# Four ring tiles in place of eight, and a selection step moved behind the last product row

## The chip, the cores and the metric

The kernel runs on one core of a Trainium2 chip. The metric is the device time of one execution in microseconds (us), the median of several runs. The core has five engines, each with its own instruction stream: TensorE (PE, its weight loads shown as PEld), VectorE (DVE), ScalarE (ACT), GpSimd (POOL) and SyncE (SP). They meet only at semaphores. Data come from HBM by DMA; here POOL issues the gathers and SP the weight loads, and the 16 DMA engines of the core carry both.

## The reference

One inference step of a two-layer decoder, for 256 prompt tokens and 32 sample tokens (288 in all, width 1024). Layer 0 mixes tokens by a short gated convolution, layer 1 by an RWKV-7 recurrence. Behind each mixer stands the same expert step, and the change lies in it alone:

```python
q = (hc @ wq).reshape(-1, 8, 256)                 # 8 heads
s1, s2 = q[..., :128] . k1,  q[..., 128:] . k2    # 128 keys each
v1, i1 = top_k(s1, 16);  v2, i2 = top_k(s2, 16)
sc, ci = top_k(v1[:, None] + v2[None, :], 16)     # 16 of 256 pairs
eidx = e1 * 128 + e2                              # one of 16384 experts
gate = softmax(sc)
z = gelu(einsum('cd,chkd->chk', hc, u_tab[eidx]))
return einsum('chk,chkd->cd', gate * z, v_tab[eidx])
```

For every token, head and choice one row of 1024 numbers is fetched from the table U and one from the table V (4 KB each). That is 288 x 8 x 16 x 2 rows in each layer.

## The kernel before

**Units.** A unit is 128 pairs of a token and a head, one per partition. Each layer has 18 units: 8 for each of two tiles of 128 prompt tokens, and 2 for the sample tokens. For a unit, choice k (0 to 15) is one gather of 128 rows of U and one of 128 rows of V, half a megabyte each. So a layer has 288 U gathers and 288 V gathers.

**Rings.** U tiles land in the ring RU, V tiles in RVV. Each holds RING = 8 tiles; choice k goes to slot k % RING. Every slot has a semaphore that says it has landed (u_land, v_land).

**The five streams of the expert step.** Unit u is the one whose V rows are in work; its U rows were handled one unit earlier, so the loops work on V of unit u beside U of unit u+1.

- POOL (L1872, get_u and get_v) issues the gathers in one fixed order: V(u,0), U(u+1,0), V(u,1), U(u+1,1), and so on. Before V(u,k) it waits until the product that used the slot last is done (v_free), before V(u,0) also for the unit's V indices (s_vidx); before U(u+1,k) it waits until the row product that used the slot last is done (s_z), before U(u+1,0) for that unit's selection (s_sel). At a layer's start it fetches the 16 U tiles of the first unit and the first RING of the second one, and then it alternates.
- DVE (unit, L1479 and on) does the row product z_of (L1449): 1024 products and their sum for each partition, of the U row and the token's h. Between the z of unit u+1 it runs the selection of unit u+2, the generator choose: 13 pieces of two instructions (maxima, indices, the grid of 256 sums), and a 14th that normalizes the gates: it waits for ACT's exponential (s_gexp), sums 16 numbers (L1429), takes the reciprocal (L1430) and scales (L1431). Two pieces stand behind each z with k = 1 to 7, so the 14th stands behind z 7. Before z 8 DVE writes the V indices of unit u+1 (v_indices, L1444). coef (L1505) multiplies gate and gelu, for 8 choices at a time.
- ACT (unit, L1098 and on) scales the V rows by their coefficients (L1114), one instruction of 128 x 1024 for each tile, in the order of k. At a unit's start it copies the scores of unit u+2 (L1104) and takes the gelu of the second eight z of unit u (L1095), before k = 10 the gelu of the first eight z of unit u+1, and before k = 13 the exponential for the gates of unit u+2 (gate_exp, L1064).
- PE (unit, L642 and on) turns each scaled V tile and adds it up in PSUM: 8 transposing products of 128 x 128 per tile (L646), and counts v_free up.
- After units 7, 15 and 17 of a layer DVE empties the PSUM sums (tile_out, L1519 and L1523).

**Around it.** SP loads weights into a ring W of its own. In layer 0 the loads for the next mixer (in_rwkv_wr) wait for the end of the last selection and so run beside the last units. The last unit has V rows alone.

Of the kernel before, what the change touches and what calls it, by code (L numbers as in the profile page):

```python
# [12 lines left out]
P = 128  # L13
D = 1024
# [4 lines left out]
TOK = NP_TOK + NS_TOK  # L19
# [3 lines left out]
HEADS = 8  # L23
NKEYS = 128
NEXP = NKEYS * NKEYS
TOPK = 16
UNITS = 18
RING = 8
WRING = 4
BANKS = 4  # L30
NEG = -3.0e38
# [88 lines left out]
def build(nc, a, out):  # L120
    with ExitStack() as ctx:
        def sb(name, shape, dt=F32):
            return ctx.enter_context(nc.sbuf_tensor(name, [P] + list(shape), dt))
# [20 lines left out]
        W = sb("W", [WRING, DC, 512])  # L144


        N_RV, N_ROWS, N_SEL = 2 * RING * D, 3 * D, 2880
        ARENA = sb("ARENA", [N_RV + 2 * N_ROWS + N_SEL])
        RV = ARENA[:, 0:N_RV]
        HTOK = ARENA[:, N_RV:N_RV + N_ROWS].rearrange("p (a d) -> p a d", a=3)  # L150
# [8 lines left out]
        gsm = sb("gsm", [2, 2])  # L159
        COUT = sb("COUT", [DC, 18])  # L160

        rings = RV.rearrange("p (r s d) -> p r s d", r=2, s=RING)
        RU, RVV = rings[:, 0], rings[:, 1]

        def carve(off, shape, dt=F32):
            n = int(np.prod(shape))
            v = ARENA[:, off:off + n]
            if dt is not F32:
                v = v.bitcast(dt)
            names = " ".join("abcd"[:len(shape)])  # L170
            return v.rearrange(f"p ({names}) -> p {names}", **{"abcd"[i]: s for i, s in enumerate(shape)})
# [12 lines left out]
        CS = carve(2 * DC * TOK + DC * UHW + DC * TOK, [DC * NS_TOK])  # L184
        CROW = carve(N_RV + N_ROWS, [D])

        KR = [carve(off, [2, HEADS, P]) for off in (RING * D + 2560, RING * D + 512)]

        Q = carve(RING * D, [16, TOK])
        KT = carve(RING * D + 16 * TOK, [2, HEADS, NKEYS])  # L190

        QP = carve(N_RV + N_ROWS, [16, P])
        HS4 = carve(N_RV + N_ROWS + 16 * P, [DC, P])
# [101 lines left out]
        s_vidx = sem("v_indices_ready")  # L295
        u_land = [sem(f"u_landed{i}") for i in range(RING)]
        v_land = [sem(f"v_landed{i}") for i in range(RING)]
# [166 lines left out]
        def _(pe):  # L464
# [72 lines left out]
            def turn_keys(layer):  # L537
                pe.wait_ge(s_keys, 16 * 2 * (layer + 1))
                for i in range(4):
                    o = group(f"kt{layer}", i)  # L540
                    for j in range(4):
                        m = pe.transpose(o[:, j * P:(j + 1) * P], KR[layer][:, i // 2, 4 * (i % 2) + j, :], ident[:])
                    done(m)
# [37 lines left out]
            def experts(layer):  # L581
# [21 lines left out]
                for h in range(2):  # L603
                    for half in range(2):
                        m = pe.matmul(o[:, (2 * h + half) * P:(2 * h + half + 1) * P], Q[:, 2 * h + half, 0:P], KT[:, half, h, :],
                                      start=True, stop=True)
# [5 lines left out]
                for tile in range(2):  # L612
                    for half in range(2):
                        for h4 in range(2):
                            o = group(f"sc{layer}", n)
                            n += 1
                            for j in range(4):
                                h = 4 * h4 + j
                                m = pe.matmul(o[:, j * P:(j + 1) * P], Q[:, 2 * h + half, tile * P:(tile + 1) * P],  # L619
                                              KT[:, half, h, :], start=True, stop=True)  # L620
                            done(m)
# [312 lines left out]
        def _(act):  # L934
# [9 lines left out]
            def load_keys(layer):  # L944
                for half, k in enumerate(("peer_k1", "peer_k2")):
                    act.dma_start(KR[layer][:, half, :, :], a[k][layer].rearrange("h k d -> k h d")).then_inc(s_keys, 16)

# [97 lines left out]
            def experts(layer):  # L1045
                squares(2 * layer + 1)
                root_and_h(2 * layer + 1)
                if layer == 0:
                    ada("ad3")
                for i in range(2):  # L1050
                    copy(f"hf{layer}", i, HTOK[:, 0, i * 512:(i + 1) * 512])

                def query(m):
                    o, free = take(f"qa{layer}", m) if m < 4 else take(f"qb{layer}", m - 4)
                    act.activation(Q[:, m, :], o[:, 0:TOK], ACT.Copy).then_inc(s_q, 1)  # L1055
                    act.wait_ge(s_q, 16 * layer + m + 1)
                    act.sem_inc(free, 1)

                u0 = layer * UNITS

                def gate_exp(u, e):

                    act.wait_ge(s_sel, u * NSEL + SEL_IDX)
                    act.activation(GATE[:, e, :], GATE[:, e, :], ACT.Exp).then_inc(s_gexp, 1)  # L1064

                for m in range(4):
                    query(m)
                o, free = take(f"se{layer}", 0)
                for e in range(2):
                    act.activation(SCUR[:, e].rearrange("p a k -> p (a k)"), o[:, 2 * e * P:2 * (e + 1) * P], ACT.Copy).then_inc(s_scur, 1)  # L1070
                act.wait_ge(s_scur, u0 + 2)
                act.sem_inc(free, 1)
                for m in range(4, 16):
                    query(m)
                    if m == GEXP_AT[0]:
                        gate_exp(u0, 0)
                    if m == GEXP_AT[1]:
                        gate_exp(u0 + 1, 1)

                for n in range(8):  # L1080
                    tile, half, h4 = n // 4, (n // 2) % 2, n % 2
                    copy(f"sc{layer}", n, SCALL[:, 8 * tile + 4 * h4:8 * tile + 4 * h4 + 4, half * NKEYS:(half + 1) * NKEYS],
                         lambda o: o.rearrange("p (h k) -> p h k", h=4))
                copy(f"sc{layer}", 8, SCALL[:, 16:18, :].rearrange("p e (a k) -> p a e k", a=2),
                     lambda o: o.rearrange("p (a e k) -> p a e k", a=2, e=2))
                for tile in range(1, 3):
                    for i in range(2):
                        copy(f"ht{layer}", 2 * tile - 2 + i, HTOK[:, tile, i * 512:(i + 1) * 512])
                for j in range(9):
                    taken(f"sc{layer}", j)  # L1090

                def gelu(u, e, half):
                    h = slice(8 * half, 8 * half + 8)
                    act.wait_ge(s_z, u * 16 + (8 * half + 8))
                    act.activation(GL[:, e, h], ZB[:, e, h], ACT.Gelu).then_inc(s_gelu, 1)  # L1095

                gelu(u0, 0, 0)

                def unit(u, lu, e, last):
                    if last == 0:  # L1100

                        act.wait_ge(s_sel, u * NSEL + NSEL)
                        act.sem_inc(s_actgo, 1)
                        act.activation(SCUR[:, e].rearrange("p a k -> p (a k)"), at(SCALL, lu + 2), ACT.Copy).then_inc(s_scur, 1)  # L1104
                    gelu(u, e, 1)
                    for k in range(TOPK):
                        if k == 10 and last < 2:
                            gelu(u + 1, 1 - e, 0)
                        if k == 13 and last == 0:
                            gate_exp(u + 2, e)  # L1110
                        if k % 8 == 0:
                            act.wait_ge(s_coef, u * 2 + (k // 8 + 1))
                        act.wait_ge(v_land[k % RING], u * 32 + 16 * (k // RING + 1))
                        act.activation(RVV[:, k % RING, :], RVV[:, k % RING, :], ACT.Copy, scale=CF[:, e, k:k + 1]).then_inc(s_scaled, 1)  # L1114

                with act.Fori(0, UNITS // 2 - 1) as i:
                    for e in range(2):
                        unit(i * 2 + (u0 + e), i * 2 + e, e, 0)
                for e in range(2):
                    unit(u0 + UNITS - 2 + e, UNITS - 2 + e, e, 1 + e)  # L1120
# [132 lines left out]
        def _(v):  # L1253
# [84 lines left out]
            for c in range(DC):  # L1338
# [5 lines left out]
                for j in range(3):  # L1344
                    k = col("conv_k", 8 * j + c)
# [88 lines left out]
            def experts(layer):  # L1434
# [10 lines left out]

                def z_of(u, k, e, h):

                    v.wait_ge(u_land[k % RING], u * 32 + 16 * (k // RING + 1))
                    v.scalar_tensor_tensor(RU[:, k % RING, :], RU[:, k % RING, :], 1.0, h, ALU.mult, ALU.mult,  # L1449
                                           accum_out=ZB[:, e, k:k + 1]).then_inc(s_z, 1)  # L1450

# [26 lines left out]
                def unit(u, lu, e, last):  # L1478

                    chosen = choose(u + 2, e, layer) if last == 0 else iter(())  # L1480
                    if last < 2:
                        for k in range(TOPK):
                            if k == 3:
                                coef(u, e, 1)
                            if k == 8:

                                v.wait_ge(s_sel, u * NSEL + 2 * NSEL)
                                v.wait_ge(v_free, u * 16 + RING)
                                v_indices(1 - e)
                            z_of(u + 1, k, 1 - e, at(HTOK, (lu + 1) // 8))  # L1490
                            if k == 14:
                                coef(u + 1, 1 - e, 0)
                            if 1 <= k < 8 or k == 15:
                                next(chosen, None)
                                next(chosen, None)
                    else:
                        coef(u, e, 1)
                    for _ in chosen:
                        pass
# [448 lines left out]
```

## Time and profile before

| | us |
|---|---|
| median of 3 runs | 2758.37 (2747.98 to 2760.15) |
| the profiled execution, its own time | 2752.55 |
| its span | 2750.8 |
| PE, DVE, POOL, ACT busy | 1985.1, 1364.6, 1311.3, 1031.9 |
| gathers, POOL's queue | 165888 packets, 604.05 MB |

Busy shares over the whole span mix stages. The two expert steps take about 840 us each (the first V gather of layer 0 starts at 326.3 us and the last at 1138.6, in layer 1 at 1909.1 and 2719.7); in them POOL and the DMA engines are busy nearly all the time, DVE and PE a good half. A row of the timeline gives start, duration, engine, line, operation and, in brackets, the idle time before it and what ended it; "issue" there is a gap in which the engine waited for nothing that the profile shows.

### The profile page before, as it was taken

What the parts mean: (1) busy time and instruction counts of PE and PEld (TensorE: products, weight loads), DVE (VectorE), ACT (ScalarE), POOL (GpSimd) and SP (SyncE); (2) the same over time, 40 slices, a digit from 0 to 9 for tenths busy, and PEclk for the clock granted to TensorE, in tenths of its full rate; (3) what the DMA queues carried; (4) which work ended last, traced back from release to release, by engine and by line L of the source; (5) the groups of instructions that cost most, each with busy time, mean ns of one, the idle gap of its engine ahead of it and who ended that gap; (6) DMA issues with size and microseconds to landing.
All of it is one profiled execution on the core that took longest, in us unless ns stands there. A gap on an engine that the chain in (4) does not pass through costs nothing.

```text
span 2750.8 us, 32207 instructions
## 1 busy us (share of the span) xinstructions
PE 1985.1 (72%) x10179; PEld 1594.1 (58%) x10179; DVE 1364.6 (50%) x3386; ACT 1031.9 (38%) x1308; POOL 1311.3 (48%) x1216
## 2 busy tenths in 40 slices
PE   6998865666666665698589897898656666666666
PEld 3676754544545544576389896567444555455455
DVE  1032655465655655323752624726465656556552
ACT  2202344444444444513211111223444444454545
POOL 2000677777777777300000000006777777777774
PEclk8899965565555555799689897899656555555556
DMA  9743899999999999724100002427999999999996
GB/s 359 289 153 124 287 363 329 361 365 367 337 360 351 367 360 392 293 95 168 38 1 1 1 1 76 115 67 249 350 347 361 351 372 347 360 362 364 356 351 243
DMA packets 242654, 717.42 MB, mean 261 GB/s; under 512 B 39672, under 2 KB 45056, under 8 KB 242556
## 3 DMA queue, kind: packets, MB, share of 16 engines
q0 software_dynamic: 165888, 604.05, 59.4%
q1 hardware_dynamic: 62212, 105.00, 10.9%
q10 hardware_dynamic: 14456, 7.06, 1.0%
q8 instruction: 61, 1.00, 0.1%
q14 instruction: 37, 0.30, 0.0%
HBM read 712.38 MB, written 3.65 MB: 260 GB/s over the span
## 4 chain that ended last, share of the span: by engine, by line
PE 35%; DMA 18%; issue 17%; DVE 13%; POOL 10%; ACT 6%; POOLq 0%; DVEq 0%; ACTq 0%; SPq 0%
PE ps L557 14%; DMA ARENA<-in_peer_v,CURV 13%; POOL ARENA L1872 10%; DVE ARENA L1449 7%; PE ps L646 5%; PE ps L774 5%; DMA ARENA<-in_peer_u,CURU 3%; ACT ARENA L1114 2%; ACT L1064 1%; PE ps L534 1%; PE ps L756 1%; PE ps L520 1%; DMA W<-in_w_ada 1%; PE ps L510 1%; PE ps L619 1%
## 5 line engine op out<-in xcount | busy, mean ns | idle before, releaser
L646 PE MATMUL ps<-ident,ARENA 128*128 128x128 f32 x4608 | 1023.3, 398 | 617.5 <-ACT ARENA L1114 616.6
L646 PEld LDWEIGHTS ps<-ident,ARENA 128*128 128x128 f32 x4608 | 833.4, 209 | 807.5 <-ACT ARENA L1114 788.3
L1872 POOL DMA_INDIRECT ARENA<-in_peer_u,CURU x576 | 642.2, 1115 | 1174.2 <-DVE ARENA L1424 978.2
L1114 ACT ACTIVATE ARENA<-ARENA,CF 128x1024 f32<-128x1024 f32 x576 | 658.1, 1147 | 769.8 <-DMA ARENA<-in_peer_v,CURV 766.6
L1449 DVE SCALAR_TENSOR_TENSOR ARENA<-ARENA 128x1024 f32<-128x1024 f32 x576 | 686.6, 1223 | 185.1 <-DMA ARENA<-in_peer_u,CURU 183.5
L1872 POOL DMA_INDIRECT ARENA<-in_peer_v,CURV x576 | 653.1, 1134 | 230.6 <-issue 152.3
L557 PE MATMUL ps<-H,W 128*128 128x288 f32 x1024 | 255.0, 412 | 3.5 <-DVEq L1801 2.8
L1429 DVE TENSOR_REDUCE gsm<-ARENA 128x1 f32<-128x16 f32 x36 | 6.1, 170 | 472.5 <-ACT ARENA L1064 472.5
L557 PEld LDWEIGHTS ps<-H,W 128*128 128x128 f32 x1024 | 197.7, 194 | 58.8 <-DVEq L1801 3.0
L967 ACT ACTIVATE W<-ps 128x512 f32<-128x512 f32 (+2 forms) x97 | 55.8, 577 | 231.4 <-PE ps L774 171.4
L967 ACT ACTIVATE ARENA<-ps 128x512 f32<-128x512 f32 (+4 forms) x106 | 55.0, 541 | 201.7 <-PE ps L557 85.2
L774 PE MATMUL ps<-W 128*128 128x128 f32 (+1 forms) x1088 | 127.6, 282 | 0.1
L557 PE MATMUL ps<-ARENA,W 128*128 128x288 f32 x512 | 127.4, 412 | 0.0
L774 PEld LDWEIGHTS ps<-W 128*128 128x128 f32 (+1 forms) x1088 | 125.5, 196 | 2.3 <-issue 0.9
L557 PEld LDWEIGHTS ps<-ARENA,W 128*128 128x128 f32 x512 | 98.7, 193 | 27.5
L1730 DVE TENSOR_TENSOR W<-W,ps 128x512 f32<-128x512 f32 (+1 forms) x76 | 50.6, 666 | 72.1 <-PE ps L774 71.3
L756 PE MATMUL ps<-ARENA 64*128 64x128 f32 (+1 forms) x480 | 59.6, 312 | 23.7 <-DVEq L1263 22.0
L756 PEld LDWEIGHTS ps<-ARENA 64*128 64x128 f32 (+1 forms) x480 | 52.5, 212 | 30.7 <-DVEq L1263 27.1
L520 PE MATMUL ps<-W,CTZ 128*32 128x512 f32 x384 | 59.4, 756 | 7.1 <-DMA W<-in_w_ada 7.1
L1552 DVE SCALAR_TENSOR_TENSOR ARENA<-ARENA,PAR,H 128x288 f32<-128x288 f32 x48 | 21.8, 514 | 82.1 <-PE ps L557 81.1
L1055 ACT ACTIVATE ARENA<-ps 128x288 f32<-128x288 f32 x32 | 13.1, 409 | 93.5 <-PE ps L557 93.3
L1449 DVE DVE_READ_ACCUMULATOR ARENA<-ARENA 128x1 f32 x576 | 46.8, 81 | 0.0
(282 smaller groups left out, 1657.6 us busy)
## 6 DMA issues: line engine op xcount, KB each, us to landing
W<-in_w_ada SPq DMA_DIRECT2D x24, 2048.0 KB, 12.6
W<-in_peer_wq SPq DMA_DIRECT2D x8, 2048.0 KB, 8.2
W<-in_conv_w_in SPq DMA_DIRECT2D x6, 2048.0 KB, 12.3
ARENA<-in_peer_u,CURU POOLq DMA_INDIRECT x576, 6.3
ARENA<-in_peer_v,CURV POOLq DMA_INDIRECT x576, 6.2
W<-in_conv_w_out SPq DMA_DIRECT2D x2, 2048.0 KB, 7.9
W<-in_rwkv_wr SPq DMA_DIRECT2D x2, 2048.0 KB, 24.0
W<-in_rwkv_wk SPq DMA_DIRECT2D x2, 2048.0 KB, 10.4
```

What stands on the lines that cost most here:

```text
L510: m = pe.matmul(o[:, m4 * NCOND:(m4 + 1) * NCOND], ADR[j % 2][:, m4 * P:(m4 + 1) * P], SELC[:], start=True, stop=True)
L520: m = pe.matmul(o[32 * q:32 * q + 32, :], CTZ[:, k, :], W[:, t % WRING, k, :], start=(k < 4), stop=(k >= 4))
L534: m = pe.matmul(o[:, 0:TOK], ones[:], SQ[:, c, :], start=(c == 0), stop=(c == DC - 1))
L557: m = pe.matmul(o[:, 0:TOK], W[:, t % WRING, k, (m0 % 4) * P:(m0 % 4 + 1) * P], rhs[:, k, :], start=(k == 0), stop=(k == DC - 1))
L646: m = pe.matmul(ps[:, acc + c // 4, c % 4 * P:(c % 4 + 1) * P], RVV[:, k % RING, c * P:(c + 1) * P], ident[:], start=(first and k == 0 and ...
L756: m = pe.matmul(o[0:n, j * n:(j + 1) * n], head(ops[0], h), head(ops[1], h), start=True, stop=True)
L774: m = pe.matmul(o[0:n, j * n:(j + 1) * n], l[:, j, :], r[:, j, :], start=True, stop=True)
L967: act.activation(dst, src(o), func, **kw).then_inc(free, 1)
L1114: act.activation(RVV[:, k % RING, :], RVV[:, k % RING, :], ACT.Copy, scale=CF[:, e, k:k + 1]).then_inc(s_scaled, 1)
L1449: v.scalar_tensor_tensor(RU[:, k % RING, :], RU[:, k % RING, :], 1.0, h, ALU.mult, ALU.mult, accum_out=ZB[:, e, k:k + 1]).then_inc(s_z, 1)
L1730: V.do(v.tensor_tensor(dst, dst, o, ALU.add))
L1872: pool.indirect_dma_start(ring[:, k % RING, :], None, tab, bass.IndirectOffsetOnAxis(ap=idx[:, k:k + 1], axis=0)).then_inc(landed[k % RING ...
```

## The change

Both rings hold four tiles in place of eight; the memory for them stays as laid out (SPAN takes the place of RING where addresses are worked out). The landing counts that ACT and DVE wait for are worked out from RING. In DVE's unit, two pieces of the selection stand behind each z with k = 1 to 6 and one behind z 7; the 14th piece, the normalization of the gates, is left to the loop behind z 15. The first row products of a layer are affected as well: `for k in range(RING)` puts 4 of them ahead of the second unit's selection, and the rest behind it; POOL fetches 4 tiles of the second unit ahead of the first V tile; PE's first count for free V slots is RING.

```diff
-RING = 8
+RING = 4
+SPAN = 8
...
-        N_RV, N_ROWS, N_SEL = 2 * RING * D, 3 * D, 2880
+        N_RV, N_ROWS, N_SEL = 2 * SPAN * D, 3 * D, 2880
...
-        rings = RV.rearrange("p (r s d) -> p r s d", r=2, s=RING)
+        rings = RV.rearrange("p (r s d) -> p r s d", r=2, s=SPAN)
...
-        KR = [carve(off, [2, HEADS, P]) for off in (RING * D + 2560, RING * D + 512)]
+        KR = [carve(off, [2, HEADS, P]) for off in (SPAN * D + 2560, SPAN * D + 512)]
...
-                        act.wait_ge(v_land[k % RING], u * 32 + 16 * (k // RING + 1))
+                        act.wait_ge(v_land[k % RING], u * (16 * TOPK // RING) + 16 * (k // RING + 1))
...
-                    v.wait_ge(u_land[k % RING], u * 32 + 16 * (k // RING + 1))
+                    v.wait_ge(u_land[k % RING], u * (16 * TOPK // RING) + 16 * (k // RING + 1))
...
                             if k == 14:
                                 coef(u + 1, 1 - e, 0)
-                            if 1 <= k < 8 or k == 15:
-                                next(chosen, None)
+                            for _ in range(2 * (1 <= k < 7) + (k == 7)):
                                 next(chosen, None)
```

## Rows read from the trace of the kernel before

**Rows 1.** Busy time of each engine in 15.75 units of layer 1 (windows)
```profile
core 0: us, PE busy (x) PEld busy (x) DVE busy (x) ACT busy (x) POOL busy (x), PEclk, DMA share, GB/s
1945.00:2685.00 740.00, 461.72 (x2013) 374.79 (x2011) 432.31 (x1148) 347.88 (x352) 565.92 (x503) 0.57 0.96 356
```

**Rows 2.** Waits in the same window: who for whom, us, times, longest
```profile
DVE gsm L1429 <- ACT ARENA L1064: 213.4, 15, 15.5
...
POOL ARENA L1872 <- DVE CURV L1444: 21.6, 14, 1.9
POOL ARENA L1872 <- PE ps L646: 18.9, 46, 2.4
```

**Rows 3.** Timeline of one unit, layer 1: a z and the gather behind it
```profile
2151.92 1.23 DVE L1449 SCALAR_TENSOR_TENSOR ARENA<-ARENA 128x1024 f32<-128x1024 f32 x1 [0.62 <-DMA ARENA<-in_peer_u,CURU]
2152.61 1.34 POOL L1872 DMA_INDIRECT ARENA<-in_peer_v,CURV  x1 [0.30 <-issue]
2158.73 1.15 ACT L1114 ACTIVATE ARENA<-ARENA,CF 128x1024 f32<-128x1024 f32 x1 [1.41 <-DMA ARENA<-in_peer_v,CURV]
2159.93 1.97 PE L646 MATMUL ps<-ident,ARENA 128*128 128x128 f32 x8 [0.59 <-ACT ARENA L1114]
```

**Rows 4.** The same unit: a gather in DVE's stall, its end, the next unit
```profile
2174.17 0.93 POOL L1872 DMA_INDIRECT ARENA<-in_peer_u,CURU  x1 [0.30 <-issue]
2179.99 0.17 DVE L1429 TENSOR_REDUCE gsm<-ARENA 128x1 f32<-128x16 f32 x1 [15.45 <-ACT ARENA L1064]
2181.93 1.03 POOL L1872 DMA_INDIRECT ARENA<-in_peer_v,CURV  x1 [1.85 <-DVE CURV L1444]
```

**Rows 5.** ACT's scalings at the end of another unit's stall, layer 1
```profile
2135.26 1.15 ACT L1114 ACTIVATE ARENA<-ARENA,CF 128x1024 f32<-128x1024 f32 x1 [1.41 <-DMA ARENA<-in_peer_v,CURV]
2137.82 1.15 ACT L1114 ACTIVATE ARENA<-ARENA,CF 128x1024 f32<-128x1024 f32 x1 [1.41 <-DMA ARENA<-in_peer_v,CURV]
```

**Rows 6.** Gathers V(1,0) and V(16,0) of layer 1, 15 units apart
```profile
1944.99 1.14 POOL L1872 DMA_INDIRECT ARENA<-in_peer_v,CURV  x1 [1.53 <-DVE CURV L1444]
...
2648.19 1.14 POOL L1872 DMA_INDIRECT ARENA<-in_peer_v,CURV  x1 [1.34 <-DVE CURV L1444]
```

**Rows 7.** The V gathers with k = 3, 8 and 11 of the unit of rows 3
```profile
2144.69 0.94 POOL L1872 DMA_INDIRECT ARENA<-in_peer_v,CURV  x1 [0.31 <-issue]
...
2158.41 1.60 POOL L1872 DMA_INDIRECT ARENA<-in_peer_v,CURV  x1 [0.31 <-issue]
...
2167.96 0.93 POOL L1872 DMA_INDIRECT ARENA<-in_peer_v,CURV  x1 [0.30 <-issue]
```

**Rows 8.** Unit 16 of layer 1, which has no selection: V(16,3), a hit, V(16,14)
```profile
2658.98 1.90 POOL L1872 DMA_INDIRECT ARENA<-in_peer_v,CURV  x1 [0.30 <-issue]
...
2679.29 1.23 DVE L1449 SCALAR_TENSOR_TENSOR ARENA<-ARENA 128x1024 f32<-128x1024 f32 x1 [1.99 <-DMA ARENA<-in_peer_u,CURU]
2679.66 1.68 POOL L1872 DMA_INDIRECT ARENA<-in_peer_u,CURU  x1 [0.30 <-issue]
...
2693.43 0.94 POOL L1872 DMA_INDIRECT ARENA<-in_peer_v,CURV  x1 [0.30 <-issue]
```

**Rows 9.** Layer 1's first V gather, and the first products
```profile
1909.07 0.93 POOL L1872 DMA_INDIRECT ARENA<-in_peer_v,CURV  x1 [5.28 <-PE ps L594]
...
1916.79 6.14 PE L646 MATMUL ps<-ident,ARENA 128*128 128x128 f32 x40 [6.80 <-ACT ARENA L1114]
```

**Rows 10.** The last unit of layer 1: V(17,0), the first scalings, the last products
```profile
2698.82 1.71 POOL L1872 DMA_INDIRECT ARENA<-in_peer_v,CURV  x1 [0.30 <-issue]
...
2706.62 9.85 ACT L1114 ACTIVATE ARENA<-ARENA,CF 128x1024 f32<-128x1024 f32 x8
...
2725.92 2.33 PE L646 MATMUL ps<-ident,ARENA 128*128 128x128 f32 x16 [0.18 <-ACT ARENA L1114]
```

**Rows 11.** Issues from 1060 to 1150 us, layer 0's last units: us to landing
```profile
W<-in_rwkv_wr SPq DMA_DIRECT2D x2, 2048.0 KB, 24.0
ARENA<-in_peer_v,CURV POOLq DMA_INDIRECT x34, 10.4
```

More of the change, by code:

```diff
@@ L185, in build @@
         CROW = carve(N_RV + N_ROWS, [D])
-        KR = [carve(off, [2, HEADS, P]) for off in (RING * D + 2560, RING * D + 512)]
-        Q = carve(RING * D, [16, TOK])
-        KT = carve(RING * D + 16 * TOK, [2, HEADS, NKEYS])
+        KR = [carve(off, [2, HEADS, P]) for off in (SPAN * D + 2560, SPAN * D + 512)]
+        Q = carve(SPAN * D, [16, TOK])
+        KT = carve(SPAN * D + 16 * TOK, [2, HEADS, NKEYS])
         QP = carve(N_RV + N_ROWS, [16, P])
```

## The prediction
> **What bounds the kernel now.** The slices of the page show the two expert steps as the long level stretches, so the view to read first is the busy time in one of them: of 740 us POOL is busy 566, DVE 432, PE 462, the DMA engines 96% [rows 1]. Two candidates, then: POOL and DMA. POOL's 503 gathers each stand 0.30 us behind the last (the gap called "issue" [rows 3]), which is 151 us more: 717 of 740 us. So POOL issues without a pause, in a fixed order, and what it is short of is time for each gather. Second view, the timeline: while DVE stands still a gather takes 0.93 us, one every 1.24, a pair of V and U every 2.48 [rows 4]. In that stretch tiles land 2.56 us apart per pair [rows 5]; that is the DMA's own pace, 1.05 MB in 2.56 us. A gather that starts while a z runs waits for it: z ends at 2151.92 + 1.23 = 2153.15, the gather at 2153.95, 0.80 us later; in unit 16 the same two ends lie 0.82 us apart [rows 3, 8]. So a gather costs 0.94 us, or what is left of the z plus 0.81.
>
> The Trainium skill (SBUF — State Buffer, Who interferes with whom) has this as a rule: a VectorE instruction with two operands in SBUF holds off a GpSimd instruction that reads SBUF, for its whole length. Rows 3 agree, with 1.34 us for 0.94. The same section infers that writing descriptors is not held off by such an instruction; by that every gather would take 0.94 us and a unit 16 x 2.56 = 41 us, where rows 6 show 46.9, so the sum doesn't use it.
>
> A unit lasts (2648.19 - 1944.99) / 15 = 46.9 us [rows 6]. Third view, the waits: DVE stands 213 us in 15 units (14.2 each) for ACT's exponential; POOL waits 21.6 us in 14 units for the V indices, written behind that stall, and hardly for free slots (18.9 us in 46, most of it the 0.30 that each gather has) [rows 2].
>
> **The change, part by part.**
>
> The moved normalization. The 14th piece waits for the exponential, which ACT does just before it scales V 13, while DVE stands behind z 7. Behind z 15 that exponential is long done: V 13 is scaled before U 15 lands. So the 14.2 us stall goes, and the V indices, no longer behind it, are there when POOL comes: 21.6 / 14 - 0.30 = 1.2 us a unit. That is all that POOL waited for. What else changes is which gathers the z hit. Before, eight z run back to back behind the stall, and the gathers beside the stall are hit by none; afterwards each z follows the landing of its tile, one for each pair. The stall was cover as well as loss, so its 14 us are not the gain. The three instructions themselves (some 0.6 us) move from one place of DVE's stream to another, where DVE is 58% busy; behind them stands z 0 of the next unit, whose tile lands later anyway.
>
> The pace with z spread out is in the trace already, since the z of k = 1 to 7 are spread out now. In the unit of rows 3 the five pairs behind V 3 take 13.72 us, 2.74 each, and the three behind V 8, hit by z that longer pieces of the selection had made late, 9.55 us, 3.18 each [rows 7]. Bounds for a pair without selection: 2.56 from below (the landings [rows 5]), 3.13 from above: in unit 16, which has neither selection nor stall, V 3 to V 14 take 34.45 us for 11 pairs, as each z falls onto the second gather behind its tile (1.68 for 0.94) [rows 8]. Unit 16 comes out of a burst of z, as no unit will; so I take the value next to rows 7, 2.77. A unit is then 3 x 3.18 + 13 x 2.77 = 45.55 us: 1.33 less, in 30 units (1 to 15 of both layers) -40 us. Unit 16 of layer 1 takes 2698.82 - 2648.19 = 50.6 us [rows 6, 10] and becomes 16 x 2.77 = 44.3: -6 us. Ends: at 2.56 for the 13 pairs -122 us, at 3.13 +100 us for the 30 units.
>
> Four tiles, between the edges. A V slot is held from the gather's start to the end of its product: 2152.61 to 2159.93 + 1.97 = 2161.90, 9.3 us [rows 3]. Four slots come round after 4 x 2.77 = 11.1 us. A U slot is held for the landing (6.1 by the V tile of rows 3), a z of 1.23 and at most a piece of selection: under 10. So the cost is nothing as long as these 1.8 us cover ACT's detours (copy, gelu and table loads at a unit's start; by the gelu's wait for z 15 some 0.5 us). If the cover is gone, each us of lateness in a slot is a quarter of a us per pair.
>
> Four tiles, first unit. POOL goes in order, so V 4 waits for product 0: it ends 1.1 us behind 1916.79, 8.8 us behind V 0 [rows 9]. Then come 12 pairs (eight before; four U tiles fewer are fetched beforehand, while POOL stood idle) at 2.77: 33.2. Sum 42.0, before 1944.99 - 1909.07 = 35.9 [rows 6, 9]: +6.1 in each layer, +12 us. Four z in place of eight ahead of the second unit's selection leave twelve behind it, whose tiles come in rounds of four; about 2 us later at the end, which layer 1 hides behind its query products and layer 0 pays by half: +1 us (0 to 3).
>
> Four tiles, last unit. Without U tiles the eight slots let V run ahead: the first V is scaled at 2706.62, the last product ends at 2728.25 [rows 10]. With four, V 4 starts at the end of product 0, about 2709.4, and V 8 and V 12 a holding time later each. Held 8.9 us (9.3, less what the light traffic saves), V 12 starts at 2727.2, V 15 at 2731.1, and the last product ends at 2740: +11.5 us. In layer 0 the weight loads (two of 2 MB, 4.19 MB at 1.05 MB in 2.56 us: 10.2 us of DMA) run beside units 16 and 17, where gathers take 10.4 us to land and queue up in the eight slots [rows 11]. With four that backlog can't form: I put +4 us on unit 16 and +6 on unit 17 (0 to 18 together).
>
> Sum, against the profiled execution's 2752.55: -40 - 6 + 12 + 1 + 11.5 + 10 = -11.5, so 2741. The median of the runs lies 5.8 us above the profiled execution; against it the forecast is 2747.
>
> **The rivals.**
>
> Faster: z slip between the gathers. A gather is held off only if it starts during a z; a z of 1.23 us that starts just behind one gather's start is over when the next one starts, 1.24 us later, hits nothing, and the pair falls to 2.56. For: all gathers in the stall show that pace when nothing hits them [rows 4, 5]. Against: the selection's longer pieces push z out of step in each unit [rows 7]. With 2.65 as the mean of the 13 pairs a unit is 44.0: 30 units at -2.9 are -87, unit 16 gives -8, the edges +34: 2697 against the median.
>
> Slower: each z falls onto the second gather. For: unit 16, ten pairs in a row [rows 8]. Against: there the landings are slow to begin with; and rows 7 don't show it. It decides from a mean of 2.80 per pair: there the units give 34 us and the edges eat them. With 3.0 a unit is 48.5: +50 in 30 units, -3 in unit 16, +34 at the edges: 2839; with 2.9 the sum is +41, 2799.
>
> Slower: four slots bind. If landing takes the 10.4 us of rows 11 for other reasons too, a slot is held 10.4 + 3.2 = 13.6 us, 3.4 per pair. Against: 9.3 us in rows 3. A holding time of 12 us gives 3.0 per pair and 2839 as above. The Trainium skill (Perfetto Trace Analysis, Optimization Strategy) says that an equal gap coming back on the engine that should be saturated can mean too little room for the next tile; POOL is that engine here, and rows 2 show no such gap with eight tiles, while no row shows four.
>
> The stall stays: DVE finds another wait for ACT in its place (the gelu before coef, or the exponential late behind z 15), the pairs keep their 46.9, and the rings cost 34 us: 2792. Against: ACT is busy 348 of 740 us [rows 1].
>
> **How the numbers follow.** Forecast 0.42 (2720 to 2775, its own range), z between the gathers 0.21, z on the second gather 0.20, slots bind 0.10, stall stays 0.07. The range that leaves out 2 in 10: 2695 to 2830. A measurement of this kernel tells about 0.5% (13.8 us) from no change. Faster than 2744.6: the second case and 0.18 of the forecast, 0.39. Within: 0.22 of the forecast and 0.04 of the slow cases, 0.26. Slower than 2772.2: 0.35.
>
> **What would show it.** Right: no wait of L1429 for L1064 above 1 us, no wait of POOL for the V indices; unit length 45 to 46 us; POOL's gathers 1.1 us in the mean; V 4 of a layer's first unit 8 to 9 us behind V 0; the last unit's products ending some 40 us behind V(17,0). Wrong: POOL waiting for products or for z in the middle of a layer (slots bind), or a mean gather above 1.2 us (z on gathers).

## The result, and the profile after

| | us |
|---|---|
| before, median of 8 runs | 2749.95 (2739.34 to 2760.15) |
| after, median of 8 runs | 2776.79 (2759.52 to 2797.89) |
| ratio | 1.0098, 95% interval 1.0063 to 1.0134 |
| the profiled execution after, its span | 2780.08, 2778.2 |

The change costs 1%. The forecast was 2747, no measurable change. The time lies inside the range that leaves out 2 in 10 (2695 to 2830) and just above the forecast's own (2720 to 2775).

First the waits, in the 15 full units of layer 1 (V(1,0) to V(16,0)) of the kernel after: who for whom, us, times, longest. Lines up to about L1490 stand one further down than before.

```profile
ACT ARENA L1115 <- DMA ARENA<-in_peer_v,CURV: 362.6, 213, 3.3
...
DVE ARENA L1450 <- DMA ARENA<-in_peer_u,CURU: 263.4, 195, 2.8
...
POOL ARENA L1872 <- issue: 144.8, 464, 1.4
POOL ARENA L1872 <- PE ps L647: 5.2, 14, 1.2
...
POOL ARENA L1872 <- DVE ARENA L1450: 2.7, 3, 1.1
```

The 213 us that DVE stood for ACT's exponential, and POOL's 21.6 us for the V indices [rows 2], are gone from the list. What DVE waits for now is the landing of its U tiles. So the moved normalization did what it says. Then why no gain? The view that tells is the busy time in the 15 full units of each layer, because POOL's busy time there is the gathers' own time (480 of them) and the rest of the window is the gaps between them. Of the kernel before, layer 0 and layer 1:

```profile
core 0: us, PE busy (x) PEld busy (x) DVE busy (x) ACT busy (x) POOL busy (x), PEclk, DMA share, GB/s
361.35:1067.62 706.27, 439.35 (x1922) 357.05 (x1921) 409.73 (x1104) 333.23 (x337) 535.65 (x480) 0.57 0.96 357
1944.99:2648.19 703.20, 439.47 (x1922) 356.91 (x1921) 410.61 (x1104) 332.82 (x337) 535.82 (x481) 0.58 0.97 358
```

And after, the same two stretches:

```profile
370.40:1067.19 696.79, 448.85 (x1922) 361.28 (x1921) 421.33 (x1104) 333.62 (x337) 541.34 (x480) 0.55 0.97 362
1967.93:2667.08 699.15, 449.04 (x1922) 361.08 (x1921) 419.68 (x1104) 333.72 (x337) 546.78 (x480) 0.55 0.97 360
```

Divided by 15, and over both layers, a unit before is 35.72 us of gathers and 11.26 us of gaps, 46.98 together; after it is 36.27 and 10.26, 46.53. The gaps gave back 1.0 us and the gathers took 0.55 of it. The forecast wanted 45.55. The 30 units give 13.5 us in place of 40, and the edges of the layers ask for more than that. These are sums of one execution each; the gathers' own time differs by 0.36 us a unit between the two layers of the kernel after alone, so the 0.55 is not far above what it does by itself. Two of these edges, read from the timeline of the kernel after (start, duration, engine, line): the first V tiles of layer 1, which answer to [rows 9], and its last unit, which answers to [rows 10].

```profile
1924.93 0.94 POOL L1872 DMA_INDIRECT ARENA<-in_peer_v,CURV  x1 [3.60 <-PE ps L595]
...
1928.66 1.94 POOL L1872 DMA_INDIRECT ARENA<-in_peer_v,CURV  x1 [0.31 <-issue]
...
1932.64 1.94 PE L647 MATMUL ps<-ident,ARENA 128*128 128x128 f32 x8 [6.80 <-ACT ARENA L1115]
1935.39 0.94 POOL L1872 DMA_INDIRECT ARENA<-in_peer_v,CURV  x1 [4.79 <-DVE ARENA L1450]
...
2711.95 1.00 POOL L1872 DMA_INDIRECT ARENA<-in_peer_v,CURV  x1 [0.30 <-issue]
...
2723.08 0.94 POOL L1872 DMA_INDIRECT ARENA<-in_peer_v,CURV  x1 [1.69 <-PE ps L647]
...
2751.80 3.22 PE L647 MATMUL ps<-ident,ARENA 128*128 128x128 f32 x16 [3.04 <-ACT ARENA L1115]
```

In the first unit V 4 starts 10.5 us behind V 0 (4.8 us of them POOL stands still; the bracket names DVE, but what that gather waits for by the program is product 0, in the row before it: that ends at 1934.58, and the gather starts 0.81 us later). In the last unit V 4 (2723.08) starts 11.1 us behind V(17,0), and the last product ends at 2755.02, 43.1 us behind V(17,0), where it was 29.4 us before. In the whole kernel after, POOL waits for a product more than 0.35 us ahead of 60 of its V gathers, and each of these starts 0.81 to 0.82 us behind the end of that product.

### The profile page after: what moved, and what is told of

Same layout as the page of the kernel before. It is cut to its first block, busy times and chain, and to the rows that moved or that the text cites. A ratio compares the mean times of both kernels' runs of the same rounds, so it can differ in the third digit from the quotient of the medians.

```text
span 2778.2 us, 32279 instructions
## 1 busy us (share of the span) xinstructions
PE 2020.8 (73%) x10179; PEld 1619.0 (58%) x10179; DVE 1386.9 (50%) x3386; ACT 1033.1 (37%) x1308; POOL 1308.9 (47%) x1216
## 4 chain that ended last, share of the span: by engine, by line
PE 31%; issue 20%; DMA 19%; POOL 16%; DVE 7%; ACT 5%; POOLq 1%; ACTq 0%; DVEq 0%; SPq 0%
POOL ARENA L1872 16%; DMA ARENA<-in_peer_v,CURV 13%; PE ps L558 11%; PE ps L647 5%; PE ps L775 5%; DMA ARENA<-in_peer_u,CURU 3%; ACT ARENA L1115 3%; DMA W<-in_w_ada 1%; PE ps L535 1%; PE ps L757 1%; DVE ARENA L1450 1%; ACT L1096 1%; DMA W<-in_conv_w_in 1%; DVE ARENA L1610 1%; DVE W L1722 1%
## 5 line engine op out<-in xcount | busy, mean ns | idle before, releaser
L647 PE MATMUL ps<-ident,ARENA 128*128 128x128 f32 x4608 | 1063.5, 409 | 601.0 <-ACT ARENA L1115 600.8
L647 PEld LDWEIGHTS ps<-ident,ARENA 128*128 128x128 f32 x4608 | 859.8, 214 | 804.3 <-ACT ARENA L1115 792.1
L1872 POOL DMA_INDIRECT ARENA<-in_peer_u,CURU x576 | 626.6, 1088 | 1190.5 <-DVE ARENA L1425 975.3
L1450 DVE SCALAR_TENSOR_TENSOR ARENA<-ARENA 128x1024 f32<-128x1024 f32 x576 | 704.0, 1224 | 625.8 <-DMA ARENA<-in_peer_u,CURU 623.7
L1872 POOL DMA_INDIRECT ARENA<-in_peer_v,CURV x576 | 666.2, 1157 | 243.5 <-issue 165.2
L757 PEld LDWEIGHTS ps<-ARENA 64*128 64x128 f32 (+1 forms) x480 | 53.7, 215 | 29.4 <-DVEq L1264 25.9
## 6 DMA issues: line engine op xcount, KB each, us to landing
W<-in_rwkv_wk SPq DMA_DIRECT2D x2, 2048.0 KB, 10.4
```

Of the source, the lines that this page charges most:

```text
L647: m = pe.matmul(ps[:, acc + c // 4, c % 4 * P:(c % 4 + 1) * P], RVV[:, k % RING, c * P:(c + 1) * P], ident[:], start=(first and k == 0 and ...
L757: m = pe.matmul(o[0:n, j * n:(j + 1) * n], head(ops[0], h), head(ops[1], h), start=True, stop=True)
L1872: pool.indirect_dma_start(ring[:, k % RING, :], None, tab, bass.IndirectOffsetOnAxis(ap=idx[:, k:k + 1], axis=0)).then_inc(landed[k % RING ...
```

## The experiments

Each ratio is to runs of the kernel before on the same chip. All variants but one keep the late normalization. In all of them `RING` is split into `UR` and `VR`, the depths of the two rings, wherever it stands; the lines shown are those that set a variant apart. The windows are of one profiled execution each.

**The normalization alone** (e1_ring8_late).

```diff
-RING = 4
+UR, VR = 8, 8
```

> Eight tiles in both rings, the normalization behind z 15. Theory A (four tiles cost time at a layer's edges alone: first unit +7 us each, last unit +9 and +14, unit 16 of layer 0 +7, first row products +4, some 49 us; in the units between the moved normalization gives 0.45 us each): all edges as before the change, units of 46.5 us, so 30 x -0.45 - 6 (unit 16 of layer 1) = -20 us against the kernel before, ratio 0.993. Rival B (four slots also hold POOL up between the edges): with eight the units fall to 45.5 or less, -50 us or more, ratio 0.98. Rival C (the late normalization gives nothing, the units vary by chance): ratio 1.00.

2710.64 us, ratio 0.9841 (0.9816 to 0.9866); profiled span 2704.5, which is 46.3 us less than before. That is the price that rival B named. So the move alone is a gain of 1.6%, and the small rings eat all of it and 1% more. The two windows of the full units:

```profile
360.60:1049.87 689.27, 446.15 (x1925) 358.52 (x1926) 419.07 (x1104) 333.81 (x337) 543.03 (x480) 0.56 0.98 365
1930.28:2609.33 679.05, 444.26 (x1925) 356.98 (x1923) 418.52 (x1104) 333.64 (x337) 532.82 (x480) 0.56 0.98 370
```

A unit: 35.86 us of gathers, as before, and 9.75 us of gaps, hardly more than 32 times the usual 0.30: no wait of POOL for anything is left. The gain is in the gaps alone, 1.5 us a unit. Between the two layers the gathers' own time differs by 0.68 us a unit (36.20 and 35.52): so much it can vary within one execution, at the same rings.

**The small rings alone** (e2_ring4_k7).

```diff
-                            for _ in range(2 * (1 <= k < 7) + (k == 7)):
+                            for _ in range(2 * (1 <= k < 8)):
```

> Four tiles in both rings, the normalization behind z 7 as before the change. Theory A: DVE stands some 14 us a unit for ACT's exponential; in that time only four U tiles can be fetched, so POOL stands at U 12 until z 8 is done, which comes about 6.1 + 1.2 + 1.5 + 1.5 + 1.2 = 11.5 us behind the start of V 12 where 1.24 us were needed: POOL waits for DVE's row products 6 to 10 us a unit, units of 53 to 57 us, some +200 to +340 us, ratio 1.07 to 1.12. Rival (the stall is cover and POOL has slack): units under 49 us, ratio below 1.04.

3147.95 us, ratio 1.1437 (1.1383 to 1.1491), more than theory A's 1.07 to 1.12. Rings of four can't stand the stall at all. From 440 to 960 us, layer 0:

```profile
DVE gsm L1430 <- ACT ARENA L1065: 132.7, 9, 16.4
...
POOL ARENA L1872 <- DVE ARENA L1450: 105.6, 11, 12.6
```

While DVE stands for the exponential no U slot comes free, and POOL stands with it, up to 12.6 us at a time. In the 30 units the waits at U 12 come to 11.1 us a unit, where 6 to 10 were expected. With eight slots the stall cost 1.5 us a unit; the pieces of this change aren't independent.

**One small ring at a time** (e3_u4_v8, e4_u8_v4).

```diff
-RING = 4
+UR, VR = 4, 8
```

The other kernel has `UR, VR = 8, 4`.

> Four U tiles, eight V tiles, the normalization behind z 15. Theory A (the last unit's price is that of the V ring; of the first unit's 7 us, 3 are V 4 standing for product 0 and 4 the U tiles that were not fetched beforehand): last units as before the change, first units +4, first row products +4 together, units of 46.5: against the kernel before 8 + 4 - 20 = -8 us, ratio 0.997. Rival (the U ring holds up the last unit or the units between as much as the V ring does): ratio above 1.005.

> Eight U tiles, four V tiles, the normalization behind z 15. Theory A: last units as after the change (+9 and +14), unit 16 of layer 0 +7, first units +3 each, first row products as before, units of 46.5: 23 + 7 + 6 - 20 = +16 us against the kernel before, ratio 1.006. Rival (the U ring makes the last unit slow): ratio below 0.998.

Four U tiles: 2714.10 us, ratio 0.9832 (0.9795 to 0.9869). Four V tiles: 2763.72 us, 1.0024 (1.0003 to 1.0045). The U ring costs nothing that shows beside the kernel with eight and eight (theory A's 0.997 took units of 46.5 us; they are 45.6); the V ring costs nearly 2% (theory A had 1.006 against the kernel before). The windows of the kernel with four V tiles:

```profile
366.87:1058.67 691.80, 442.87 (x1924) 356.54 (x1923) 420.54 (x1104) 333.58 (x337) 538.00 (x480) 0.56 0.97 364
1957.87:2653.76 695.89, 447.45 (x1917) 359.76 (x1918) 419.51 (x1104) 333.70 (x337) 540.46 (x480) 0.55 0.97 362
```

Against eight and eight the units cost 2.5 us more in layer 0 and 16.8 us more in layer 1 (gaps 10.31 us a unit in place of 9.75 in the mean of both). Of the 56.9 us between the two spans the rest, some 37 us, is at the edges: the two first units take 82.7 us in place of 73.5, unit 16 of layer 0 54.0 in place of 44.3, the last units 68.8 in place of 49.4 from V 0 to V 15. Nearly all of this was in the forecast's terms for the edges.

**What POOL waits for in the middle** (e8_gelu_later with rings of four and four, e9_u8_v4_gelu with U eight and V four). In the kernel after, POOL stands at V 4 in 14 of the 30 units, 8.1 us beyond the usual 0.30. One of them, layer 0:

```profile
417.13 0.99 POOL L1872 DMA_INDIRECT ARENA<-in_peer_v,CURV  x1 [0.30 <-issue]
...
421.09 1.15 ACT L1115 ACTIVATE ARENA<-ARENA,CF 128x1024 f32<-128x1024 f32 x1 [1.53 <-DMA ARENA<-in_peer_v,CURV]
...
422.26 1.28 ACT L1105 ACT_TABLE_LOAD   x1
...
423.55 0.42 ACT L1105 ACTIVATE ARENA<-W 128x256 f32 x1
...
423.99 1.28 ACT L1096 ACT_TABLE_LOAD   x1
...
425.39 1.13 ACT L1115 ACTIVATE ARENA<-ARENA,CF 128x1024 f32<-128x1024 f32 x1
...
426.58 1.97 PE L647 MATMUL ps<-ident,ARENA 128*128 128x128 f32 x8 [2.32 <-ACT ARENA L1115]
...
429.36 0.94 POOL L1872 DMA_INDIRECT ARENA<-in_peer_v,CURV  x1 [1.90 <-DVE ARENA L1450]
```

Between two scalings ACT loads two tables, for the score copy and for the gelu: 422.24 to 425.39, 3.15 us. The tile of V 0 (first row) has landed at 423.60, so its scaling is some 1.8 us late, and product 0 and V 4 with it. Product 0 ends at 428.55, and again the gather that waits for it starts 0.81 us later, 12.2 us behind V 0. Every second unit has both loads, the others the gelu's alone; 12 of the 14 waits stand in units with both. The kernel before has the same two loads between two scalings, in layer 1 for example here:

```profile
2092.78 1.28 ACT L1104 ACT_TABLE_LOAD   x1
2094.07 0.42 ACT L1104 ACTIVATE ARENA<-W 128x256 f32 x1
2094.51 1.28 ACT L1095 ACT_TABLE_LOAD   x1
2097.44 0.21 ACT L1095 ACTIVATE GL<-ZB 128x8 f32<-128x8 f32 x1 [1.65 <-DVE ARENA L1449]
```

In the two experiments the gelu is put behind the scaling of V 2:

```diff
-                    gelu(u, e, 1)
                     for k in range(TOPK):
+                        if k == 3:
+                            gelu(u, e, 1)
```

> The changed kernel with ACT's gelu of a unit's second eight z behind the scaling of V 2 in place of the unit's start. Theory A (V 4 stands for product 0 in every second unit because ACT loads tables, copies scores and takes the gelu before it scales V 0): POOL's waits at V 4 go from 8 us in 30 units to under 2, pair V 3 to V 4 from 3.04 to about 2.85 us, units from 46.5 to about 46.2: -6 to -12 us against the changed kernel, ratio to the kernel before 1.006. Rival (the late product 0 has another cause): the waits at V 4 stay, ratio 1.01.

> U ring of eight, V ring of four, late normalization, and the gelu at a unit's start moved behind the scaling of V 2. Theory A: part of what the V ring of four costs in the middle is that V 4 stands for a product 0 made late by two table loads in ACT; then the units fall from the 46.1 and 46.4 us of the same kernel with the gelu in its old place to about 45.7, POOL's waits over 0.35 us at V 4 nearly go, and the ratio falls by some 0.5 % from 1.002, to 0.997. Theory B: the V ring of four costs at the edges of a layer and by how z and gathers fall in with each other, and the waits at V 4 are only time that POOL would lose elsewhere; then the ratio stays 1.002.

Four and four: 2772.29 us, ratio 1.0086 (1.0052 to 1.0119), where the kernel after has 1.0098. Eight and four: 2759.62 us, 1.0016 (0.9999 to 1.0033), where the kernel with the gelu in its old place has 1.0024. The waits at V 4 fall as they should (from 8.1 us in 14 units to 1.2 us in 4; from 6.3 us in 10 to 0.7 us in 3). So their cause is shown. What they are worth in time is not: by the ratios the two kernels gain some 3 us, give or take 13, and 2 us, give or take 7. That rules out the 14 us that theory A named for the second one; it doesn't rule out the 7 and 6 us that the waits themselves came to. The windows, first of four and four, then of eight and four:

```profile
371.88:1060.10 688.22, 453.20 (x1925) 362.61 (x1924) 420.76 (x1104) 333.96 (x337) 536.98 (x480) 0.55 0.98 366
1962.34:2649.69 687.35, 446.44 (x1921) 357.56 (x1921) 419.51 (x1104) 334.35 (x337) 537.85 (x480) 0.56 0.98 366
...
367.53:1060.09 692.56, 448.40 (x1922) 358.54 (x1921) 420.76 (x1104) 333.48 (x337) 542.32 (x481) 0.56 0.98 364
1956.78:2651.21 694.43, 454.26 (x1926) 363.10 (x1924) 419.35 (x1104) 334.61 (x337) 543.50 (x480) 0.55 0.97 362
```

With four and four a unit is 45.85 us, the mean of both layers, 0.68 less than in the kernel after: the gaps fall by 0.24 and the gathers' own time by 0.44. (The profiled execution is the fastest of that kernel's four, 2762.84 us.) With eight and four the gaps fall to 10.04 us, 0.27 less than with the old place, and the gathers' own time rises to 36.19, 0.24 more; the sum stays. So the same edit goes with shorter gathers in one kernel and with longer ones in the other. A pause at V 4 shifts the gathers against the z, and that may move their time, but no run shows that it does.

**The z taken off the gathers** (e6_psum8, e5_psum4, e10_psum_u4_v8). The disputed cost by itself: for the units from the second one of a layer, the z reads the token's h from PSUM, where PE has transposed it once per tile; ring depths eight and eight, four and four, four and eight. All else is computed as before. In the last line `h` stands for the tile's banks of `ps`.

```diff
+                def h_in_psum(tile):
+                    for c in range(DC):
+                        src = H[:, c, tile * P:(tile + 1) * P] if tile < 2 else HS4[:, c, :]
+                        m = pe.transpose(ps[:, 2 * (tile % 2) + c // 4, c % 4 * P:(c % 4 + 1) * P], src, ident[:])
+                    m.then_inc(s_hps, 1)
...
-                            z_of(u + 1, k, 1 - e, at(HTOK, (lu + 1) // 8))
+                            z_of(u + 1, k, 1 - e, h)
```

> Eight tiles in both rings, the normalization behind z 15, and the token's h for the row products of units 1 to 17 read from PSUM (PE turns h into banks 0 to 3, which lie idle in the units), so that a z has one operand in SBUF in place of two. Theory A (what a late pair costs over 2.48 us is gathers held off by z, because z reads two operands from SBUF): gathers take 0.94 us beside z as well, POOL's unit is 39.7 us, the DMA's 41, a unit 41 to 42 where eight tiles alone gave 45.6; against the kernel before 31 x -5.5 = -170 us, ratio 0.935 to 0.945. Rival (z holds gathers off whatever it reads, or the DMA's pace sets the unit): units stay at 45 to 46 us, gathers beside z at 1.2 us and more, ratio 0.98 to 0.99.

> The same with four tiles in both rings. Theory A: the pairs come at 2.56 us, four slots go round in 10.2 us, a slot is held 9.3 and ACT's work at a unit's start takes 2 to 3 us more every second unit, so V 4 stands for product 0 in most units: units of 42.5 to 44 us, edges +45: ratio 0.96 to 0.975. Rival (four slots are enough at any pace): units as with eight tiles, only the edges lost, ratio 0.955 or less.

> h for the row products in PSUM, U ring of four, V ring of eight. Theory A: four U tiles are enough at the faster pace too, since the transfers set the pace and a tile only waits longer in their queues when there are more of them; then the units are 40.6 us as with eight and eight, and the ratio is 0.93. Theory B: four U slots bind, since a U tile was issued 14 to 15 us ahead of its row product with eight slots and four come round in 10.1 us; POOL then waits for row products, the units are above 41.5 us, and the ratio is 0.94 to 0.96, as with four and four.

First a hit as it is in the kernel after, layer 1: a z, and the V gather that starts inside it.

```profile
2001.82 1.22 DVE L1450 SCALAR_TENSOR_TENSOR ARENA<-ARENA 128x1024 f32<-128x1024 f32 x1 [1.97 <-DMA ARENA<-in_peer_u,CURU]
...
2002.19 1.66 POOL L1872 DMA_INDIRECT ARENA<-in_peer_v,CURV  x1 [0.30 <-issue]
```

And two gathers that start inside a z in the kernel with h in PSUM and rings of eight:

```profile
512.24 1.22 DVE L1466 SCALAR_TENSOR_TENSOR ARENA<-ARENA,ps 128x1024 f32<-128x1024 f32 x1 [1.34 <-DMA ARENA<-in_peer_u,CURU]
...
512.72 0.94 POOL L1891 DMA_INDIRECT ARENA<-in_peer_u,CURU  x1 [0.30 <-issue]
...
514.79 1.22 DVE L1466 SCALAR_TENSOR_TENSOR ARENA<-ARENA,ps 128x1024 f32<-128x1024 f32 x1 [1.32 <-DMA ARENA<-in_peer_u,CURU]
...
515.20 0.93 POOL L1891 DMA_INDIRECT ARENA<-in_peer_u,CURU  x1 [0.30 <-issue]
```

The z takes 1.22 us as ever, and a gather that starts 0.48 or 0.41 us into it takes 0.94 and ends 0.20 or 0.12 us after the z, no longer 0.81. None of these gathers waits for that z by a semaphore, and yet it held them off with both inputs in SBUF: engines meet elsewhere than at semaphores too. Eight and eight: 2556.99 us, ratio 0.9291 (0.9271 to 0.9311), the fastest kernel of the study. Its windows:

```profile
356.82:965.07 608.25, 407.18 (x1904) 331.21 (x1903) 412.98 (x1098) 327.68 (x334) 452.31 (x480) 0.65 1.03 409
1847.23:2455.15 607.92, 413.39 (x1905) 334.87 (x1904) 413.01 (x1098) 327.51 (x334) 452.91 (x480) 0.63 1.03 409
```

A unit is 40.54 us: 30.17 of gathers (0.943 each) and 10.37 of gaps. The collisions of z and gathers cost 5.7 us a unit (35.86 less 30.17), of which 0.62 come back as gaps, since the DMA engines are now what POOL is early for. This shows in the time from issue to landing, in layer 0 first from 356 to 397 us and then from 680 to 965 us:

```profile
ARENA<-in_peer_v,CURV POOLq DMA_INDIRECT x17, 8.8
...
ARENA<-in_peer_v,CURV POOLq DMA_INDIRECT x111, 16.0
```

In units 1 to 7 of both layers POOL goes at its own pace, 39.9 us a unit, and the tiles queue up; when the eight slots are full, it waits for them, and units 8 to 15 take 41.1 us. Tiles land 2.56 us apart for each pair, in the median, and 16 times that is 41.0. With four and four: 2644.06 us, 0.9605 (0.9579 to 0.9631).

```profile
371.17:1003.48 632.31, 424.51 (x1929) 343.74 (x1929) 418.17 (x1104) 332.12 (x337) 453.86 (x481) 0.61 1.01 398
1898.91:2536.58 637.67, 424.25 (x1929) 342.42 (x1930) 417.81 (x1104) 333.13 (x338) 453.35 (x481) 0.62 1.01 395
```

Here the gathers' own time is the same, 30.2, and the gaps are 12.1: with the collisions gone four slots bind, 1.7 us a unit. Four U and eight V tiles: 2570.46 us, 0.9327 (0.9297 to 0.9358), units of 41.2. So the V ring costs most here too, 2.8% of the time before, and the U ring some 0.4%: neither theory of that run was quite right, four U tiles bind a little (POOL waits at U 9 in 19 of the 30 units, 10.4 us beyond the usual 0.30 in all). Eight and eight came out below theory A's 0.935 to 0.945, four and four at the low end of its theory A.

The Trainium skill (SBUF — State Buffer, Who interferes with whom) says that a VectorE instruction with at most one input in SBUF, outside its two-port modes, doesn't contend with GpSimd, and that one with two contends with a GpSimd instruction that reads SBUF. These two pairs of rows agree (1.66 and 0.94 us). Its inference, drawn there for `tensor_tensor`, that descriptor writing stays clear of such an instruction, was set aside by the prediction, and rightly for these gathers: their time changed with where the z's second input lay. A gather also reads its indices from SBUF; whether the reading or the writing is held off, no run shows.

## Why the prediction was wrong

Its terms, against the profiled executions (2750.8 and 2778.2 us of span; units from V 0 to V 0, first row products from the first U gather to V 0 in both layers, the last unit to the end of its last product):

| term | predicted | measured |
|---|---|---|
| 30 units | -40 | -13.5 |
| unit 16 of layer 1 | -6 | -5.8 |
| first unit, both layers | +12 | +14.6 |
| first row products | +1 | +3.9 |
| last unit of layer 1 | +11.5 | +13.6 |
| layer 0, units 16 and 17 | +10 | +16.8 |
| everything else | 0 | -2.2 |
| sum | -11.5 | +27.4 |

**What bounds the kernel: right.** POOL's order of gathers, each 0.94 us or what is left of the z and 0.81 more; in the pair above the gather ends at 2003.85 and the z at 2003.04, 0.81 apart. And 2.56 us a pair is the DMA's pace: tiles land at it with h in PSUM, and the units there take 16 times that once the slots are full.

**The moved normalization: right, with its size.** The forecast without its ring terms is -40 and -6; the normalization alone gave -46.3 us of span. Its units take 45.61 us; 45.55 were predicted. Both sides of the argument held: the stall goes, and its 14 us a unit are not the gain, as the gathers' own time stays (35.72 and 35.86 us).

**The step that failed is "Four tiles, between the edges", whose cost was "nothing".** It took 9.3 us as the time a V slot is held, compared it with 11.1 us for four slots to come round, and let the 1.8 us between them cover ACT's detours, put at 0.5 us. Two terms of that were wrong. In every second unit the detour at the unit's head is 3.15 us, and the scaling of a tile that has landed is late by 1.8 in the unit shown; the rows of the kernel before had those loads too. And a slot isn't free for POOL when its product ends: the gather that waits for it starts 0.81 us later, which the sum left out. Together that is more than the cover, and POOL waits for products in the middle of a layer, which was one of the text's signs of being wrong.

The units of the change take 46.53 us, 0.92 more than with rings of eight, 27.6 us in 30 units. Against the forecast the 30 units are 26.5 of the 38.9 us by which the sum was off. Of the 27.6, 15.3 us are POOL's waits for slots, which the kernel with eight and eight hasn't at all: 8.1 at V 4, mostly behind ACT's detour, the rest spread over V and U. The other 12.4 us are gathers that took longer, 0.41 us a unit; as the gathers' own time differs by 0.68 us between two layers of one execution, that part may be chance, and its cause is open.

The mean of the 13 pairs without longer selection pieces is 2.85 us, 2.77 were predicted, and the text put the point at which the edges eat the gain at 2.80. At 2.85 its own sum gives 30 x 13 x 0.08 = 31 us more, 2778, which is the time measured, but by luck: the sum stood on a median before of 2758, where eight runs gave 2750, and its terms for the edges were 12 us too small. So the kernel came close to two of its rivals, z onto the second gather and four slots that bind, each in a small measure, and neither at the price named (2839).

**The edges: right in kind, low in size.** V 4 of a layer's first unit stands 10.5 us behind V 0, where 8.8 were taken from product 0 as it was. The sum gave product 0 1.1 us, from a row of five products merged into one; by itself it takes 1.94 us, in the kernel before as well:

```profile
1916.79 1.94 PE L646 MATMUL ps<-ident,ARENA 128*128 128x128 f32 x8 [6.80 <-ACT ARENA L1114]
```

The 0.81 us from its end to the gather come on top, and the two make up the whole difference. The last unit of layer 1 has the 0.81 us in each round of the ring, and there V 13 to V 15 wait for products too, where the sum let them follow V 12 at once. In layer 0, V tiles land in 6.2 us beside the weight loads, where it was 10.4 [rows 11]. That is the backlog that can't form, as predicted; the price of units 16 and 17 was 16.8 us, within the 18 given as the upper end, but not the 10 chosen. Issues from 1060 to 1150 us, after:

```profile
W<-in_rwkv_wr SPq DMA_DIRECT2D x2, 2048.0 KB, 27.3
ARENA<-in_peer_v,CURV POOLq DMA_INDIRECT x32, 6.2
```

**What stays open.** What sets how many gathers meet a z: their own time changes from layer to layer and from kernel to kernel by several tenths of a us a unit, the shift of one against the other moves with every wait, and no run fixed it alone. And why the U ring costs nothing that shows beside eight V tiles (ratios 0.9832 and 0.9841), but 0.7%, some 20 us, beside four (1.0098 and 1.0024).

## What to carry to other kernels

A ring's depth is to be compared with the longest time that a slot is held, table loads and detours of every engine on its way and the step from the last engine to the next gather included, not with the time in one quiet pair; and at each edge of a loop it is paid again. A stall taken off an engine that isn't the bound is worth only the gap it makes on the engine that is, and that gap can be read beforehand. When the bounding engine's own instructions are sometimes longer than their shortest form, look for what lengthens them first: here that was worth 5.5% (0.9841 to 0.9291), the stall 1.6%.

## What the runs showed of the hardware

The DMA engines' busy share of 0.96 to 0.98 was not their ceiling: it went to 1.03 while the rate rose from 358 to 409 GB/s, 14%. There the median time from issue to landing of a gather was 14.8 us over the whole kernel, where it was 6.1 in the kernel after, at a better rate: POOL issued a pair in 2.49 us and the tiles landed 2.56 us apart, so they only waited longer in their queues. A long time to landing was no sign of slow transfers here. A gather that waited for a product started 0.81 to 0.82 us behind that product's end, in all 60 cases of the kernel after. And the run-to-run spread went with the collisions: the runs of the three kernels with h in PSUM lie within 2.0, 3.5 and 6.6 us, those of the kernel before within 21 and of the kernel after within 38; that the shift of z against gathers makes this spread is likely, but wasn't tested by itself.
